# Moving the V/K-token and gate stage of an mLSTM head into its chunk-scan loop

## The reference

```
h = rms_norm(x); proj = h @ w_in           # u_a, z_a, q, k, v, o, z_b, gates, g_a, g_b
q, k = silu(centred_depthwise_conv([q, k], width 5))
# per head and direction, chunk by chunk:
scores = (q_c @ k_c.T) * decay_mask
num    = scores @ v_c + inter_scale * (q_c @ C)     # C: 256 x 256 state
den    = sum(scores) + inter_scale * (q_c @ n)      # n: 256 state
h_c    = num / max(|den|, exp(-m))
C, n   = keep * C + kw_c.T @ v_c,  keep * n + sum(kw_c)
# both directions are summed, RMS-normed per head,
y_b = hb * sigmoid(o) * silu(z_b)
```

## Time and profile before

| | |
|---|---|
| median of 2 runs | 2798.9 us (2790.2 to 2807.59) |
| profiled execution | 2808.92 us, span of its slowest core (core 4) 2807.4 us |
| spans of the 8 cores | 2762.5 to 2807.4 us |
| granted TensorE clock, mean of the span | 0.867 to 0.880 of 2.4 GHz |
| busy share of the span | TensorE 74%, VectorE 40%, ScalarE 38%, GpSimd 14% |

### The profile page before, as it was taken

The page is one execution under the profiler, slowest core; times in us unless marked ns, Lnnn a source line. Parts: engine busy times, 40 slices in busy tenths (PEclk is TensorE's granted clock), DMA queues, the critical chain, the costliest instruction groups (busy, mean ns, idle before and its releaser), DMA issues.

```text
span 2807.4 us, 42508 instructions; the slowest of 8 cores (2762.5 to 2807.4 us)
## 1 busy us (share of the span) xinstructions
PE 2089.0 (74%) x11536; PEld 1064.0 (38%) x11632; DVE 1116.9 (40%) x3017; ACT 1053.4 (38%) x2595; POOL 391.7 (14%) x558
## 2 busy tenths in 40 slices
PE   0288678687668599788792685977859769988986
PEld 0235335335325253333342353443534425433432
DVE  1336536536536412423423146263462622244243
ACT  3335525526515432212114247374473723111121
POOL 0001201201201201221211003020030200122122
PEclk9997688687769699999995797987979879999998
DMA  8244452565564204334434110010100021344343
GB/s 206 97 91 64 80 84 64 124 140 118 128 135 82 68 9 156 120 129 142 137 114 156 38 39 1 1 39 1 39 1 1 2 68 53 121 150 144 127 142 105
DMA packets 221961, 246.81 MB, mean 88 GB/s; under 512 B 117537, under 2 KB 139041, under 8 KB 221601
## 3 DMA queue, kind: packets, MB, share of 16 engines
q1 hardware_dynamic: 205090, 224.65, 29.8%
q0 software_dynamic: 4608, 16.78, 1.5%
q10 hardware_dynamic: 12032, 2.66, 0.4%
HBM read 201.54 MB, written 42.50 MB: 87 GB/s over the span
## 4 chain that ended last, share of the span: by engine, by line
PE 53%; DMA 13%; DVE 12%; issue 9%; ACT 8%; SPq 1%; DVEq 1%; POOL 1%; ACTq 1%; POOLq 0%
PE ps L346 51%; DVE arena L327 6%; ACT arena L309 5%; DMA arena<-w_in 4%; DMA wsc<-arena 4%; ACT arena L331 3%; DMA arena<-wsc 2%; PE ps L351 2%; DVE arena L333 2%; DVE arena L319 2%; DVE arena L312 2%; DMA arena<-x 1%; DVEq L158 1%; POOL arena L312 1%; DMA arena<-w_out 1%
## 5 line engine op out<-in xcount | busy, mean ns | idle before, releaser
L346 PE MATMUL ps<-arena 128*128 128x512 bf16 (+5 forms) x10768 | 2011.2, 341 | 433.2 <-DVE arena L312 132.5
L346 PEld LDWEIGHTS ps<-arena 128*128 128x128 bf16 x10864 | 1000.9, 103 | 1417.2 <-issue 695.3
L327 DVE SCALAR_TENSOR_TENSOR arena<-arena,ps 128x512 f32<-128x512 f32 (+2 forms) x960 | 485.4, 539 | 874.0 <-PE ps L346 418.9
L312 POOL TENSOR_TENSOR arena<-arena 128x128 bf16<-128x128 bf16 (+3 forms) x480 | 355.3, 752 | 2165.6 <-ACT arena L309 1197.2
L309 ACT ACTIVATE arena<-ps 128x512 f32<-128x512 f32 (+2 forms) x640 | 272.5, 426 | 759.3 <-PE ps L346 663.8
L309 ACT ACTIVATE arena<-ps,arena 128x128 bf16<-128x128 f32 (+2 forms) x640 | 280.4, 470 | 426.3 <-PE ps L346 368.4
L331 ACT CAST arena<-ps 128x512 bf16<-128x512 f32 (+1 forms) x352 | 179.2, 509 | 357.2 <-PE ps L346 308.7
L351 PE MATMUL ps<-arena 128*128 128x128 bf16 x768 | 112.4, 272 | 266.7 <-DVE arena L319 151.5
L319 DVE TENSOR_SCALAR arena<-arena 128x128 bf16<-128x128 f32 (+5 forms) x465 | 167.0, 394 | 266.2 <-DMA arena<-w_in 173.1
L309 ACT ACTIVATE arena<-arena 128x256 bf16<-128x256 bf16 (+4 forms) x462 | 217.3, 501 | 76.5 <-DVE arena L319 23.5
L327 DVE SCALAR_TENSOR_TENSOR arena<-arena 128x1 f32<-128x1 f32 (+3 forms) x540 | 184.0, 346 | 137.6 <-ACT arena L309 75.7
(11 more groups left out here) (16 smaller groups left out, 124.0 us busy)
## 6 DMA issues: line engine op xcount, KB each, us to landing
arena<-wsc SPq DMA_DIRECT2D x64, 1024.0 KB, 5.8
arena<-x SPq DMA_DIRECT2D x64, 512.0 KB, 7.1
arena<-w_in SPq DMA_DIRECT2D x160, 128.0 KB, 3.5
arena<-wsc SPq DMA_DIRECT2D x8, 2560.0 KB, 11.0
arena<-w_in SPq DMA_DIRECT2D x64, 256.0 KB, 3.7
arena<-wsc SPq DMA_DIRECT2D x64, 256.0 KB, 3.0
y<-arena POOLq DMA_DIRECT2D x32, 512.0 KB, 5.8
wsc<-arena SPq DMA_DIRECT2D x112, 128.0 KB, 2.5
```

Source lines behind the costliest of these rows:

```text
L312: sc.add(eng, lambda e: e.tensor_tensor(out.ap, a.ap, b.ap, op), reads=[a, b], writes=[out])
L327: sc.add(eng, lambda e: e.scalar_tensor_tensor(out.ap, a.ap, sa, bap, op0, op1), reads=r, writes=[out])
L346: ins = e.matmul(out.ap, l.ap, rh.ap, start=(i == 0), stop=(i == n - 1))
```

## The change

The body of the V/K/gate stage becomes a function vstage(t). `ensure(j)` calls it for tile j and for tile 15 - j if they are not done. Before the scan ensure(0) and ensure(1) run, four tiles. The other twelve are done in the scan loop: `ensure(i + 2)` stands in iteration i between the Abs of the denominators and the state update, and finds two tiles to do in iterations 0 to 5 and none later. The conversion steps of sequence 0 move with their tiles.

To run beside the scan the stage is given other PSUM banks: V and the K transposes both in bank 5, the gate in bank 4 alone (before: V in 4 and 5, K in 6, gate in 7 and 3). In the scan psN moves from bank 5 into bank 0, where psS is, and psNum has three banks (6, 7, 1) in place of four.

```diff
--- before.py
+++ after.py
@@ -623,29 +623,39 @@
                         stt("dve", dst, tb, 1.0, pb, ALU.add, ALU.mult)
                         if sq == 0:
                             sprinkle()
-                for t in range(NT):
+                def vstage(t):
                     tc_ = slice(t * 128, (t + 1) * 128)
-                    pb = psv(4 + t % 2)
-                    mm(pb[:, 0:256], [(xT[:, c, tc_], wh[:, 4:6, c, :]) for c in range(8)])
-                    cp("act", vtok[:, t, 0:256], pb[:, 0:256])
-                    pk = psv(6, BF16)[:, (t % 4) * 256:(t % 4) * 256 + 256]
+                    pvk = psv(5)
+                    mm(pvk[:, 0:256], [(xT[:, c, tc_], wh[:, 4:6, c, :]) for c in range(8)])
+                    cp("act", vtok[:, t, 0:256], pvk[:, 0:256])
+                    pk = psv(5, BF16)[:, 512:768]
                     for j in range(2):
                         tr(pk[:, j * 128:(j + 1) * 128], kT2[:, j, tc_], identb)
                     cp("dve", ktok[:, t], pk)
-                    pgate = psv(7 if t % 2 == 0 else 3)
+                    pgate = psv(4)
                     mm(pgate, [(xT[:, c, tc_], wh[:, 6:10, c, :]) for c in range(8)])
-                    tb = tnh[t % 2]
+                    tb = tnh[len(vdone) % 2]
                     act(tb, pgate, AF.Tanh, scale=0.5)
-                    a_ = ga_[t % 2]
+                    a_ = ga_[0]
                     stt("dve", a_, tb[:, 256:512], 1.0, pgate[:, 256:512], ALU.add, ALU.mult)
                     stt("dve", gate_all[:, t], tb[:, 0:256], 1.0, a_, ALU.add, ALU.mult)
                     if sq == 0:
                         sprinkle()
+                vdone = set()
+                def ensure(j):
+                    for dr_ in range(2):
+                        t_ = j if dr_ == 0 else NT - 1 - j
+                        if t_ not in vdone:
+                            vdone.add(t_)
+                            vstage(t_)
+                ensure(0)
+                if NT > 1:
+                    ensure(1)
                 memset("pool", Cst[1], 0.0); memset("pool", nst[1], 0.0); memset("pool", Cb[1], 0.0)
                 psS = [psv(0)[:, 0:128], psv(0)[:, 128:256]]
                 psP = [psv(2), psv(3)]
-                psN = [psv(5)[:, 0:2], psv(5)[:, 64:66]]
-                numbanks = [psv(6), psv(7), psv(1), psv(4)]
+                psN = [psv(0)[:, 256:258], psv(0)[:, 320:322]]
+                numbanks = [psv(6), psv(7), psv(1)]
                 NB_ = len(numbanks)
                 def cflat(v_):
                     return V(v_.ap.rearrange("p a b -> p (a b)"), "sb", v_.off, [128, 512], [0, 4], 4)
@@ -713,6 +723,8 @@
                            [(qT2[:, c, tc_], cbr[:, dr, c]) for c in range(2)])
                     for dr in range(2):
                         act(dn2[i % 2][:, dr], psNum[dr][:, 256:257], AF.Abs)
+                    if i + 2 < NT:
+                        ensure(i + 2)
                     for dr in range(2):
                         stt("dve", cflat(Cst[i % 2][:, dr]), cflat(Cst[(i + 1) % 2][:, dr]), g_dec[:, dr, i, h:h + 1],
                             psP[dr], ALU.mult, ALU.add)
```

## The result

The changed kernel takes 3145.98 us (median of 11 runs, 3131.6 to 3292.86) against 2800.16 us in the same sessions: ratio 1.1232, 95% interval 1.1206 to 1.1257. Its profiled execution has a span of 3150.8 us on core 7. The forecast was 3200 in a range of 3055 to 3270. A median here is over all executions, of which some run a few per cent longer at a lower clock on some cores; the ratios and their intervals leave those out.

A forecast was written before the change was run, and what follows sets the result against it. TensorE was taken to bound the V/K/gate stage, ScalarE the scan's first half. Profiled 2808.9 + 25 (banks) + 252 (place) + 110 (clock) + 13 (late iterations) = 3210, less 10 for the median: 3200 us, range 3055 to 3270.

The forecast's parts named there:

- rival 2: Iterations 0 to 5: tiles and scan run serially but the clock holds, 3089 us; chance 0.20.
- Banks of the vstage: V/K/gate tiles: transposes wait for ScalarE's V copy, 0.77 us a tile; 25 us for the four ahead of each scan.
- The place in the loop: Iterations 0 to 5: state update waits behind both vstages, TensorE behind it; 13.9 us against 8.72, 252 us in all.
- The clock: Iterations 0 to 5: V matmuls begin at 1.2 GHz and run so for 4 us; 2.3 us x 48 = 110 us.
- Iterations 6 to 15: Late scan without vstages: psS written only after the state update, 0.55 us in 6 and 7, 0.1 in five others; 13 us.
- Rival 1: Iterations 0 to 5: state update slips in beside the vstages, filling TensorE's idle time; saves 47 us, 2752 or 2790; chance 0.09.

The follow-up runs named there:

- e2: Kernel before the change, with only the vstage's banks changed (V and K transposes share bank 5, gate alone in bank 4): 2905.77 us, ratio 1.0360.
- e5: Changed kernel with 12 matmuls that nobody reads added in TensorE's idle time behind the second gate matmuls of each of 48 iterations: 3095.27 us, ratio 1.1086.
- e7b: Kernel before the change, with only psN moved to bank 0 and four num banks kept: 2823.56 us, ratio 1.0116.
- e8: Kernel before the change, with only psNum reduced to three banks and psN left in bank 5: ratio 1.0115.
- e6b: Changed kernel with iterations 0 to 5 reordered, state update before the second gate product, psN alone in bank 1: 2793.76 us, ratio 0.9975 to the kernel before.
- e10: e6b with the cast of n recorded as its four single elements instead of one view: 2766.09 us, ratio 0.9894 to the kernel before.

## Why the prediction was right, and where its sizes were off

The time lay in the range, though halfway between the forecast and rival 2, both of which the range took in. The mechanism is the one that was forecast, at its place: the gap behind VectorE in each of the iterations, the state update right behind the gate product, the wait for the psS reads behind it. Going by its steps:

- *Banks of the vstage.* Forecast 3.48 us a tile and 25 us in the four ahead of the scan; measured 3.50, and e2 shows the same for all 16.
- *The place in the loop.* Forecast 13.9 us at full clock; e5, in which the clock is full, has 13.50. The idle time was 3.5 for 3.9 us, in part because the state update begins 0.34 us after the second gate product does (1827.40 - 1827.06), overlapping it, where the sum let it wait for its end, 0.53.
- *The clock: the step that was mis-sized.* Forecast 2.3 us an iteration, 110 us in all; e5 puts it at 1.06, 41 to 51 us. The sum let the V matmuls begin at 1.2 GHz and run so for 4 us, from the row 1920 to 1930 of the earlier trace rows. But that stretch followed 20 us of sparse work in the kernel before. In the loop the clock falls before the V matmuls come, 0.75 us into stage_s, and mostly for 3.4 us, so that the scan's small matmuls are slow together with the first V matmuls; when the gate matmuls come it is mostly back at 1.00. The term was also added up too high: its own pieces are 0.87 for V, 0.63 for the gate matmuls (1.25 + 1.11 - 1.73) and 0.11 for the transposes, 1.6 us in place of 1.75. The granted clock over iterations 0 to 5 was foretold as 0.6 to 0.8 and is 0.80 to 0.85 over the eight heads.
- *Iterations 6 to 15.* Forecast 13 us, measured 12.0 + 9.7 = 21.7. The sum priced the 0.55 us of psS alone: e7b, which has only that, takes 5.8 + 6.1 = 11.9 us more in these columns. e8 shows that the third num bank costs as much again, 6.8 + 5.7 = 12.5 us, a wait that the sum had counted in iterations 0 to 5 and forgotten here.

In sum 400 us were forecast and 346 came: clock 60 too much, late iterations 9 too little, the rest a little too much. Rival 2 (the clock holds, 3089) was off by about as much on the other side. Rival 1 has its answer in e6b and e10: the idle time can be filled, from the point that was named (the state update starts before the second gate's matmuls end), and what comes is 30 us by the ratio (32.7 in the table) of the 47 that it had to give. The Trainium skill says in "Perfetto Trace Analysis", section Optimization Strategy, that regimes with different bounds may gain by interleaving. e10 agrees (0.9894), and the changed kernel (1.1232), on the same pair of regimes, shows that the gain depends on the order.

## What to carry to other kernels

When a stage is moved into a loop, follow it through every in-order queue, not only the one that is to be filled: what stands first on VectorE must be what the recurrence needs, and the moved work comes behind it. Take PSUM banks away only after pricing each alone in the unmoved kernel: here they cost 164 us before anything was interleaved, part of it through a lower granted clock. And when an operation waits for something it doesn't read, look at the extent that was recorded for the other one's view.

## What the runs showed of the hardware

With 3.5 us of idle time in a period of 14.3 us, TensorE's granted clock fell to half once in each iteration, and not in the idle time itself (1.00) but 0.75 us behind it; it was back after 3.4 us (6.8 in one of the five), so that the dense part ran mostly at 1.00. With the idle time filled by useless matmuls it stayed at 1.00 in these windows, and the kernel was 41 to 51 us faster.
